# SBUF tiles moved by multiples of 64 bytes: four spacer tiles shrunk or removed in a two-network float32 kernel

## The reference

```python
def first_block(x, c, ...):          # two layers
    for l in range(2):
        h = h + 0.5 * gate * _swiglu(modulate(rmsnorm(h)), ffn_w_in[l, 0], ffn_w_out[l, 0])  # 1024 -> 2816 -> 1024
        z = modulate(rmsnorm(h)) @ mix_w_in[l]
        y_a = _nsa(q, k_*, v_*, gates, ...)      # sparse attention, 8 heads of 64
        y_b = _gmlp(zuv, ...)                    # gating within chunks of 128 positions
        h = h + gate * ((sigmoid(zga) * (y_a @ proj_a[l]) + sigmoid(zgb) * (y_b @ proj_b[l])) @ w_out[l])
        h = h + 0.5 * gate * _swiglu(modulate(rmsnorm(h)), ffn_w_in[l, 1], ffn_w_out[l, 1])
    return rmsnorm(h)

def second_block(x, ctx, ...):       # x: 512 positions, ctx: 256 positions
    # layer 0: pooling mixer and MLP (1024 -> 4096 -> 1024) on both x and ctx
    # layer 1: attention of x over ctx and x (8 heads of 128), then the MLP on x
```

## The kernel before, in words

| tiles | first byte, for the first of them | byte within its 128-byte line |
|---|---|---|
| raw, WH, WL, araw, cB, scr, h (left, ahead of "line") | 17536 (raw0), 33920 (WH0) | 0 |
| ident, ones | 119360, 119872 | 64 |
| nH, nL; rows; hH, hL; gH, gL (right) | 212864, 196480; ...; 180096, 163712; 204160 | 0 |
| yaH, yaL, q, ko, ks, Vt, P, PT, ybH, ybL, mH, mL; ma, hH2, hL2 (left, behind "line") | 130688 (yaH), 163456 (mH) | 0 |
| nHc | 139328 | 64 |
| nLc, hHc, hLc, mid, fin | 152128, 160320, 168512, 176704, 184896 | 64 |
| nHk; nLk | 188096; 130688 | 64; 0 |

## Time and profile before

### The profile page before, as it was taken

The page is one execution under the profiler, slowest core; times in us unless marked ns, Lnnn a source line. Parts: engine busy times, 40 slices in busy tenths (PEclk is TensorE's granted clock), DMA queues, the critical chain, the costliest instruction groups (busy, mean ns, idle before and its releaser), DMA issues.

```text
span 3464.7 us, 46915 instructions
## 1 busy us (share of the span) xinstructions
PE 3413.6 (99%) x18494; PEld 2874.5 (83%) x18494; DVE 2165.7 (63%) x3570; ACT 1318.4 (38%) x1951; POOL 298.0 (9%) x376
## 2 busy tenths in 40 slices
PE   9999999999999999999999999999999999999998
PEld 7888967898888988896789888899988898588888
DVE  7555565656555655666577777888776556655444
ACT  4222463333222422245333523355533236643222
POOL 0000232001000100023100000012100001210000
PEclk9999999999999999999999999999999999999999
DMA  7444302434444344320243444344444311013221
GB/s 279 188 158 163 107 24 101 163 129 168 158 162 151 134 169 158 148 106 12 101 164 140 149 150 170 146 147 182 172 174 165 117 66 68 25 50 112 96 98 48
DMA packets 85561, 452.01 MB, mean 130 GB/s; under 512 B 10304, under 2 KB 12544, under 8 KB 48608
## 3 DMA queue, kind: packets, MB, share of 16 engines
q1 hardware_dynamic: 83168, 439.10, 34.2%
q0 software_dynamic: 2176, 9.92, 0.8%
HBM read 446.88 MB, written 2.10 MB: 130 GB/s over the span
## 4 chain that ended last, share of the span: by engine, by line
PE 84%; DVE 7%; ACT 3%; issue 2%; DMA 2%; POOL 0%; SPq 0%; DVEq 0%; ACTq 0%; POOLq 0%
PE ps L662 21%; PE ps L663 21%; PE ps L664 21%; DVE WL L568 2%; DMA araw<-in_ast 2%; PE ps L2778 1%; PE ps L2780 1%; PE ps L2779 1%; PE ps L3477 1%; PE ps L1039 1%; PE ps L1040 1%; PE ps L1041 1%; ACT P L1859 1%; PE ps L1776 1%; PE ps L1299 1%
## 5 line engine op out<-in xcount | busy, mean ns | idle before, releaser
L662 PE MATMUL ps<-nH,WH 128*128 128x512 f32 x2256 | 880.3, 390 | 0.4 <-ACT rot L3207 0.4
L664 PE MATMUL ps<-nH,WL 128*128 128x512 f32 x2256 | 877.8, 389 | 0.0
L663 PE MATMUL ps<-nL,WH 128*128 128x512 f32 x2256 | 877.8, 389 | 0.0
L568 DVE TENSOR_TENSOR WL<-raw,WH 128x2048 fp32r<-128x2048 f32 (+2 forms) x297 | 651.6, 2199 | 361.5 <-ACT WH L557 360.0
L557 ACT ACTIVATE WH<-raw 128x2048 fp32r<-128x2048 f32 (+2 forms) x299 | 543.2, 1822 | 561.1 <-PE ps L664 479.9
L662 PEld LDWEIGHTS ps<-nH,WH 128*128 128x128 f32 x2256 | 423.5, 188 | 90.6 <-issue 3.3
L664 PEld LDWEIGHTS ps<-nH,WL 128*128 128x128 f32 x2256 | 423.4, 188 | 88.3
L663 PEld LDWEIGHTS ps<-nL,WH 128*128 128x128 f32 x2256 | 423.5, 188 | 87.2 <-issue 0.2
L628 DVE SCALAR_TENSOR_TENSOR araw<-araw,cB 128x1024 f32<-128x1024 f32 x224 | 275.6, 1230 | 205.6 <-DMA araw<-in_ast 205.2
L662 PE MATMUL ps<-hH,WH 128*128 128x512 f32 x944 | 368.8, 391 | 2.5 <-DVE ma L2454 1.4
L664 PE MATMUL ps<-hH,WL 128*128 128x512 f32 x944 | 367.4, 389 | 0.0
(11 more groups left out here) (452 smaller groups left out, 5940.0 us busy)
## 6 DMA issues: line engine op xcount, KB each, us to landing
raw<-in_wst SPq DMA_DIRECT2D x273, 1024.0 KB, 4.8
araw<-in_ast SPq DMA_DIRECT2D x225, 512.0 KB, 5.7
raw<-in_wst SPq DMA_DIRECT2D x18, 512.0 KB, 3.3
araw<-in_wst SPq DMA_DIRECT2D x9, 1024.0 KB, 4.8
row<-in_ast SPq DMA_DIRECT2D x15, 512.0 KB, 10.5
cw<-in_cw POOLq DMA_DIRECT2D x4, 1024.0 KB, 5.9
h<-in_xT SPq DMA_DIRECT2D x4, 512.0 KB, 5.6
raw<-in_wst SPq DMA_DIRECT2D x8, 256.0 KB, 2.6
```

Source lines behind the costliest of these rows:

```text
L568: dve.q.tensor_tensor(M.WL[k % NW][:, 0:n], M.raw[raw_use[k]][:, 0:n], M.WH[k % NW][:, 0:n].bitcast(F32), ALU.subtract).then_inc(*v_wlo.up(k))
L662: pe.q.matmul(to, hi[:, i, cc], xh, start=i == 0, stop=False)
L663: pe.q.matmul(to, hi[:, i, cc], xl, start=False, stop=False)
L664: t = pe.q.matmul(to, lo[:, i, cc], xh, start=False, stop=i == nk - 1)
```

## The change

The pad at the right end shrinks from 96 to 32 bytes and the three other spacer tiles go. Nothing else is touched: the same instructions with the same shapes, waits, order and queues, at other addresses.

```diff
@@ def memory(nc, ctx)
     M.h = sb(ctx, "h", [128, KT, S])
-    sb(ctx, "pad", [128, 24], side="right")
+    sb(ctx, "pad", [128, 8], side="right")
     lat, con, key = Space(), Space(), Space()
...
     with ExitStack() as ph:
         M.hH = sb(ph, "hH", [128, 2, 4, S], F32R, side="right")
         M.hL = sb(ph, "hL", [128, 2, 4, S], F32R, side="right")
-
-    sb(ctx, "line", [128, 16])
...
     M.xc = sb(cx, "xc", [128, KT, C])
     with ExitStack() as bc:
-        sb(bc, "lines7", [128, 16 * 7])
         con.nH = sb(bc, "nHc", [128, KT, C], F32R)
         con.scr = [sb(bc, f"scrc{i}", [128, C + 16]) for i in range(4)]
         con.rs = sb(bc, "rsc", [128, 16])
-        sb(bc, "lines3", [128, 16 * 3])
         with ExitStack() as bp:
             M.hpc = sb(bp, "hpc", [128, KT, C + 16])
         con.nL = sb(bc, "nLc", [128, KT, C], F32R)
```

## The result

The changed kernel takes 3484.51 us (median of 4 runs, 3482.98 to 3492.92), the kernel before 3465.84 us beside it. The ratio, taken over seven executions of the changed kernel, is 1.0059, with an interval of 1.0045 to 1.0074: slower, by 18.7 us between these medians and by some 20 us by the ratio. The forecast was slower by 41.3 us.

What follows compares the result with a forecast made beforehand. The prediction took TensorE's own matmul pace to bound the kernel. Terms of 49.1 - 10.4 + 1.8 + 0.8 = +41.3 us on 3466.5 gave 3507.8 us, or 3507 on the median's level; range 3432 to 3518 us.

Steps and rivals of the forecast that it cites:

- What bounds the kernel: Whole kernel: TensorE is busy 3413.6 of 3464.7 us, its longest wait entry 9.0 us, so its own pace sets the time.
- So the start address within 128 bytes goes with the pace: 256-column matmuls: 120.2 ns at byte 0 of a 128-byte line, 117.8 ns at byte 64.
- the reading by the line: Large products: the moving operand's byte within its 128-byte line, 0 or 64, was taken to set the matmul pace.
- at 256 columns byte 64 means out of step: Context stage: 256-column matmuls at byte 64 run at 117.8 ns, never settling, in all but a small part.
- Out of step: 512-column matmuls at byte 64 stay at the 231.5 ns seen behind stops, +4.8 ns each; chance 0.50, 3507 us.
- 512 columns: Main products, 10224 matmuls going from byte 0 to byte 64: +4.8 ns each, +49.1 us; bounds -71 and +68 us.
- 256 columns: Main products, 4320 matmuls going from byte 0 to byte 64: -2.4 ns each, -10.4 us; bounds -30 and 0.
- Context: Context stage: hHc and hLc to byte 0, 768 matmuls, +1.8 us; nHc mixed with nLc, 768 matmuls, +0.8 us.
- Plain and bf16 matmuls, writes of ScalarE and VectorE: Some 2300 short matmuls: 0, bounds 2 us each way; writes to moved tiles: 0 on the path, bounds to 16 us.
- Differs between stretches behind different stops: Sign of error: a 512-column pace that varies this way would mean the forecast's explanation of the paces is incomplete.
- the phase reading: Matmul streams behind stops start at an arbitrary phase of something periodic (6.67 ns) and fall into step after some ten matmuls.
- the step higher: Rival: 512-column matmuls settle one 6.67 ns step up at 233.3 ns, +68 - 7.8 us, 3527 us; chance 0.10.

Runs made afterwards that it cites:

- all_shifted: Kernel before with right-hand tiles, raw, WH, WL and all other left-hand tiles up by 64 bytes together: 3464.97 us, ratio 0.9999.
- weights_only: Kernel before with WH and WL shifted up by 64 bytes, moving operands of the main stages in place: 3513.71 us, ratio 1.0142.
- right_256: Kernel before with the right-hand pad at 224 bytes, moving right-hand tiles down by 128 bytes to distance 128: 3510.99 us, ratio 1.0131.
- wl_64: Kernel before with dummy allocated in front of WL, so WL goes up by 64 bytes while WH stays: 3502.22 us, ratio 1.0106.
- right_32: Kernel before with the right-hand pad at 64 bytes, putting right-hand tiles at distance 32: 3513.19 us, ratio 1.0139.
- right_rel96: Kernel before without the right-hand pad, putting right-hand tiles at distance 96: 3519.27 us, ratio 1.0154.
- right_96: Kernel before with the right-hand pad at 128 bytes, putting right-hand tiles at distance 224: 3517.31 us, ratio 1.0152.
- right_only: Kernel before with only the right-hand pad cut from 96 to 32 bytes, right-hand tiles at distance 64: 3480.14 us, ratio 1.0043.
- left_only: Kernel before with only left-hand tiles moved to distance 192 (line removed, lines7 grown, context in place): 3469.07 us, ratio 1.001.

## Why the prediction was right in sign and wrong in size

**What bounds the kernel: right.** TensorE's own pace set the time, and waits stayed as they were. The loss lies in start distances. Taken matmul by matmul over the two traces, which hold the same 18494 in the same order, the distances between starts grew by 29.2 us in the 512-column products, shrank by 10.8 in those of 256 columns and grew by 2.1 in the context's. Stops and all other matmuls together changed by less than 0.4 us. That is the 20.3 us between the spans.

**The failed step** is the one that begins "So the start address within 128 bytes goes with the pace". The earlier trace rows compare context tiles with main tiles. They differ in the byte within the line, and also in the distance to the weights. The forecast took the first for the cause, and all_shifted (3464.97 us), weights_only (3513.71) and right_256 (3510.99) show that it was the second. With the reading by the line went the step "at 256 columns byte 64 means out of step", and so the choice of 231.5 ns for all 10224 matmuls. The context's rows were at distance 192, while 8688 of those 10224 went to distance 64. The kernel before held no 512-column matmul at any distance but 0, and distance 64 only in nHk of the short key stage.

**"Out of step" was misread too.** The forecast took 117.8 ns for a pace that never falls into step, as it is no multiple of 6.67 ns. Three matmuls in a row, one for each product, take 353.4 ns at that pace, and that is 53 times 6.67. In the same way three take 680 ns at 226.7 (102 times), 686.7 at 228.9 (103), 693 in wl_64 (104) and 700 at 233.3 (105). So the steady stretches at 117.8 and 228.9 ns keep a step too, one of three matmuls, and the 231 and 232 ns behind a stop were the wrong row for their pace.

**The terms, re-made with the measured paces.**
- 512 columns, right: 8688 x (228.9 - 226.7) = +19.1 us. Left: 1536 x (233.3 - 226.7) = +10.1 us. Together +29.2, forecast +49.1. This term was mis-sized, and it is where the error lies: 20 of the 23 us. The forecast pace of 231.5 ns is found at neither distance. It is near neither the 228.9 ns of most of the work nor the 233.3 ns of the rest.
- 256 columns: 4320 x -2.4 = -10.4 us, as forecast. This was luck in part: the forecast value came from tiles at distance 192, and 2784 of the 4320 went to distance 64, where the pace happens to be 117.8 ns as well. mH at 117.9 ns is the forecast value, with one stretch at 113.9, which the bounds covered.
- Context: hHc and hLc at 120.0 ns as forecast, 768 x 2.1 = +1.6 us. It came out right under both readings, since the tiles went to byte 0 and to distance 0. nHc with nLc, forecast +0.8, reads 282 ns instead of 283, and between starts nHc took 0.55 us less and nLc 0.55 us more: nothing.
- Sum: 29.2 - 10.4 + 1.6 = +20.4 us, against 20.3 between the two spans and 18.7 between the medians.
- Plain and bf16 matmuls, writes of ScalarE and VectorE: 0 was right. All other matmuls together changed by 0.4 us between starts. The write into hH takes 633 ns and into hL 687, both as in the earlier trace rows:

```profile
L1149 ACT ACTIVATE hH<-scr 128x512 fp32r<-128x512 f32 x152 | 95.7, 633 | 362.3 <-DVE scr L1195 360.3
...
L1204 DVE TENSOR_TENSOR hL<-scr,hH 128x512 fp32r<-128x512 f32 x152 | 100.7, 687 | 4.3
```

**The signs the forecast asked for.** "Differs between stretches behind different stops" was named as what would make the phase reading incomplete, and that came: 228.8 and 233.3 ns for nH. At 228.8 ns, 302 us hold about 1321 starts, where 1306 were forecast. That the sign came out right was luck in part: it rested on the pace behind stops, and nothing in the kernel before showed a 512-column matmul at distance 64 or 192. Among the rivals, the step higher (233.3 ns) is what five of the seven other distances do, and what the left-hand tiles did. Had all main tiles gone there, weights_only shows the price: +49.1 us, where its rival had +60. The difference lies at 256 columns: at distance 192 many of those stretches run at 113.3 ns and not at 117.8. Between starts, weights_only gained 19.1 us at 256 columns, not 10.4, and lost 66.2 at 512.

**The two pages.** The Trainium skill (TensorE: Matmul & The Clock Gate, "Wait — 56ns, not 53.3ns?") gives N/2.4 GHz plus about 2.5 ns for warm back-to-back matmuls, with no term for an address. That would be 512/2.4 + 2.5 = 215.8 ns, an estimate by that page. The runs give 226.7 to 234.4 ns, by the distance. The Trainium skill (SBUF — State Buffer, "Door 1: The DMA port swizzle") names lines of 16 bytes as what a read pays for. Every shift here is a multiple of 16 bytes, so by that rule none would matter. The runs disagree: a shift by 32 bytes cost 48.6 us (right_32).

## What to carry to other kernels

Before moving tiles in SBUF under a stream of back-to-back matmuls, write down for each moving operand its start minus that of its weights, modulo 256 bytes. For 512-column float32r matmuls 0 was the best of the eight distances tried in this kernel. Moving the weights counts as much as moving the data. When two rows of a trace are compared to find what an address does, list everything in which they differ, here the place in the line and the distance to the weights, and ask whether the change goes to a value that the trace holds at all. A spacer tile that nothing reads can be worth 1.5% of the time (right_rel96 has no pad on the right).

## What was not expected of the hardware

- The steady start distance of 512-column single-pass float32r matmuls depends on the distance between moving operand and weights: 226.7 ns at 0, 228.9 at 64 (and some 233 in one stretch), 233.3 to 233.5 at 32, 96, 128, 192 and 224, 234.4 at 160. A shift of data and weights together by 64 bytes does nothing (all_shifted).
- At 256 columns the order is another: 120.0 to 120.2 ns at 0, 117.8 at 64, and 117.8 or 113.3 at 192. Taken between starts, most stretches of nH and hH run at 116.7 ns at 32 (right_32), 120.0 at 96 (right_rel96), 118.9 at 128 (right_256) and 118.3 at 224 (right_96). The best distance for the one width is not the best for the other.
- A stretch can carry over something of what runs before it: in right_only the unmoved ya and yb, 24 matmuls at a time between stretches of nH at distance 64, take 227.7 to 228.8 ns between starts, at distance 0, where the kernel before has 226.7.
- At distance 192 a 256-column stretch takes one of two paces, and which one changes between kernels that have the same distances (mH: 113.3 ns in left_only, 117.9 in the changed kernel).
- One product of three off its distance costs twice its share (wl_64: 13 ns per three matmuls instead of 6.6).
- Three matmuls in a row, one of each product, mostly take a whole number of times 6.67 ns: 102, 103, 104 or 105 times at 512 columns, 51, 53 or 54 at 256. Some distances keep to other values, 105.5 times at 160 (512 columns, 703.3 ns) and 53.5 at 128 (256 columns, 356.7 ns).
- What has the period of 256 bytes, and what the 6.67 ns are, stays open. No run here looks inside it.
